# Block 1's seven-product units: three of the four weight sums made in DRAM by accumulating DMAs

## The chip, the cores and the metric

One core of one Trainium2 chip. The metric is device time of one execution, in microseconds (us).

## The reference, cut to what matters

Block 1 runs twice (l = 0, 1): a mixing part (latent attention "mla", a dilated attention "dil", a neighbourhood attention "nbr", gates, output projection) and then the feed-forward that the change is about. Block 2 follows and isn't touched.

```python
D_MODEL, SEQ, DEPTH = 1024, 512, 2
D_FF = 2816                      # 22 x 128
for l in range(DEPTH):
    ...                          # mixing part
    x = x + merged @ w_o[l]
    h = rms_norm(x, g_ffn[l])
    x = x + (jax.nn.silu(h @ w1[l]) * (h @ w3[l])) @ w2[l]
```

All is fp32. The kernel splits each operand in a high and a low part (fp32r) and makes a product as three matmuls: high x high, high x low, low x high.

## The kernel before, in words

**Engines and queues.** The program is written as one straight list per engine (TensorE, ScalarE, VectorE, GpSimd, SyncE); each executes its own in order, and waits on semaphores. A wait holds everything behind it on that engine.

**Weights.** All weights of the program lie in DRAM in one array `in_wts` of loads of 128 x 1024 (512 KB), in the order of use. SyncE loads them into slots of `s_raw` (2, and 4 in the feed-forward), each when its slot has been given back. A chunk is 1024 columns: ScalarE copies it to `wh` (high part, L611), VectorE subtracts to get `wl` (low part, L670), TensorE uses both. There are 3 slots of `wh` and `wl` (RING = 3), so chunk c can only be split when TensorE is done with chunk c - 3. `upto(L, c)`, `ahead()` and `weights()` say at which point of its list an engine puts the split of a chunk.

**The feed-forward of block 1.** 22 units i of 128 hidden columns. `KINDS` says how each is computed: 0 to 3 "U" (on the unnormalised x), 4 and 5 "N" (plain, on the normalised x: 48 matmuls of 512 columns each), 6 to 21 "S": the seven-product form, in which gate and up projection (w1 and w3, halves a and b of the 1024 inputs) share products over half of the tokens, 84 matmuls of 256 columns where a plain unit has 48 of 512. Units 0 to 10 come first, then half of w2 (`h_h`, `h_l` in the trace), then units 11 to 21, then the other half of w2.

An S unit has four chunks, made of two loads a = [w1a, w3a] and b = [w3b, w1b]:

- chunk 0: `s_b` = [w1a + w3a, w3a + w3b] (sum S1, 1024 wide, GpSimd, L714)
- chunk 1: [w1a, S2], with S2 = w1a + w3a + w3b, written over w3a in `s_raw` (512 wide, GpSimd, L714)
- chunk 2: w1b, 512 wide
- chunk 3: [w3b, S4], with S4 = S2 + w1b (512 wide, VectorE, L660, `s_raw<-s_raw`)

It needs four token sums too (`n_ta`, `n_tb`, split into `zh` and `zl`), made once per layer between the N units. GpSimd also makes the product of gate and up (`f_t<-f_t`, L714) of each U and S unit. In a unit ScalarE has in this order: copy c1, split of chunk 3, copy s1 (both copies write `s_s`); TensorE's product P2 waits for s1. Chunk 3's split waits for S4.

**The MLA loop.** 41 steps; in the first 32 TensorE makes a tile of scores, VectorE its minimum (L1427) and reciprocal (L1252), ScalarE the exponential (L614, `m_p<-bank`), GpSimd the scaling (`m_p<-m_p`, L717), and three steps later TensorE transposes that tile (L355). After it comes the dilated loop, 13 steps twice, whose first scaling on GpSimd is `b_p<-b_p` (L717).

## Time and profile before

| | us |
|---|---|
| median of 3 runs | 3257.82 (3256.49 to 3259.09) |
| the profiled execution | 3259.56 |
| its span in the trace | 3257.9 |

| engine | busy us | share |
|---|---|---|
| TensorE | 3203.1 | 98% |
| VectorE | 2030.9 | 62% |
| ScalarE | 1400.4 | 43% |
| GpSimd | 775.7 | 24% |

PE is TensorE, PEld its weight loads, DVE VectorE, ACT ScalarE, POOL GpSimd, SP SyncE. A matmul's end is modelled, so what counts is the distance from start to start. A share of busy time is a mean over stages with different limits; a hole in TensorE's row is read with the engine that released it, which stands in brackets. 40 slices of the span show a granted TensorE clock of 90% or more in each.

### The profile page before, as it was taken

The numbers are of one execution on the slowest core, as the hardware profiler recorded it, in microseconds if no ns is written. First come the engines' busy times: TensorE is split into PE (matmuls) and PEld (weight loads), VectorE is DVE, ScalarE is ACT, GpSimd is POOL, SyncE is SP. The second block draws the span as 40 slices with busy tenths as digits, with TensorE's granted clock in tenths as the row PEclk, the third lists the DMA queues.
The fourth block names the chain that finished last, engine by engine and source line by source line (L and its number), as shares of the span: only waits on it lengthen the run. The fifth ranks groups of instructions, "written<-read, shape, count | busy, mean of one in ns | idle before, by whom it ended". The sixth has DMA issues, their size and how long they took to land.

```text
span 3257.9 us, 41235 instructions
## 1 busy us (share of the span) xinstructions
PE 3203.1 (98%) x16588; PEld 2727.8 (84%) x16588; DVE 2030.9 (62%) x2980; ACT 1400.4 (43%) x2175; POOL 775.7 (24%) x562
## 2 busy tenths in 40 slices
PE   9999999999999999999999999999999999999998
PEld 7888888788888888888888888888888898788887
DVE  6865775777848655846949665554544268974433
ACT  5653553344437634633424433332423248843221
POOL 1521241223304311520325022110211013521101
PEclk9999999999999999999999999999999999999999
DMA  4122323232231122222222322222232222223322
GB/s 136 48 74 68 107 94 101 82 110 91 85 115 55 64 72 93 102 97 97 99 90 91 107 81 81 88 84 91 91 103 91 101 85 93 91 91 100 101 97 84
DMA packets 85150, 295.78 MB, mean 91 GB/s; under 512 B 9568, under 2 KB 12128, under 8 KB 84960
## 3 DMA queue, kind: packets, MB, share of 16 engines
q1 hardware_dynamic: 84384, 292.76, 27.0%
q8 instruction: 131, 2.15, 0.3%
q14 instruction: 59, 0.48, 0.0%
q10 hardware_dynamic: 576, 0.40, 0.0%
HBM read 291.02 MB, written 2.10 MB: 90 GB/s over the span
## 4 chain that ended last, share of the span: by engine, by line
PE 78%; DVE 13%; ACT 4%; issue 3%; POOL 2%; DMA 0%; SPq 0%; ACTq 0%; POOLq 0%; DVEq 0%
PE bank L352 77%; DVE wl L670 5%; PE bank L355 2%; ACT wh L611 1%; DVE s_raw L660 1%; ACT m_p L614 1%; DVE small L1427 1%; POOL f_t L714 1%; POOL u_g L714 1%; DVE f_t L660 1%; DVE u_uc L666 0%; DVE m_ptl L670 0%; DVE h_l L673 0%; DMA s_raw<-in_wts 0%; DVE m_qf L660 0%
## 5 line engine op out<-in xcount | busy, mean ns | idle before, releaser
L670 DVE TENSOR_TENSOR wl<-s_raw,wh 128x1024 fp32r<-128x1024 f32 (+1 forms) x563 | 734.1, 1308 | 552.2 <-ACT wh L611 551.1
L352 PE MATMUL bank<-zh,wh 128*128 128x512 f32 (+1 forms) x2588 | 946.9, 366 | 5.7 <-ACT zh L611 5.7
L352 PE MATMUL bank<-zh,wl 128*128 128x512 f32 (+1 forms) x2588 | 942.4, 364 | 5.0 <-DVE wl L670 5.0
L352 PE MATMUL bank<-zl,wh 128*128 128x512 f32 (+1 forms) x2588 | 939.8, 363 | 1.7 <-DVE zl L673 1.6
L611 ACT ACTIVATE wh<-s_raw 128x1024 fp32r<-128x1024 f32 (+1 forms) x563 | 575.1, 1028 | 550.2 <-PE bank L352 410.1
L352 PEld LDWEIGHTS bank<-zh,wl 128*128 128x128 f32 x2588 | 489.1, 189 | 88.7 <-DVE wl L670 11.4
L352 PEld LDWEIGHTS bank<-zh,wh 128*128 128x128 f32 x2588 | 489.6, 189 | 80.2 <-ACT zh L611 5.7
L352 PEld LDWEIGHTS bank<-zl,wh 128*128 128x128 f32 x2588 | 489.3, 189 | 75.8 <-DVE zl L673 3.0
L714 POOL TENSOR_TENSOR f_t<-f_t 128x512 f32<-128x512 f32 x84 | 118.1, 1406 | 524.7 <-DVE f_t L666 524.7
L720 POOL TENSOR_TENSOR small<-small 128x1 f32<-128x1 f32 (+3 forms) x35 | 43.0, 1229 | 822.1 <-DVE small L663 822.1
L352 PE MATMUL bank<-n_h,wh 128*128 128x256 f32 (+1 forms) x448 | 136.9, 306 | 24.9 <-ACT s_s L611 17.6
L352 PE MATMUL bank<-f_mh,wh 128*128 128x512 f32 (+1 forms) x396 | 146.4, 370 | 0.0
L352 PE MATMUL bank<-wh,zh 128*128 128x512 f32 (+2 forms) x384 | 145.1, 378 | 1.0 <-ACT b_qk L611 1.0
L714 POOL TENSOR_TENSOR s_b<-s_raw 128x1024 f32<-128x1024 f32 x32 | 84.7, 2645 | 256.2 <-DMA s_raw<-in_wts 219.8
L352 PE MATMUL bank<-f_mh,wl 128*128 128x512 f32 (+1 forms) x396 | 145.3, 367 | 0.0
L352 PE MATMUL bank<-f_ml,wh 128*128 128x512 f32 (+1 forms) x396 | 144.2, 364 | 0.0
L352 PE MATMUL bank<-wh,zl 128*128 128x512 f32 (+2 forms) x384 | 143.8, 375 | 0.0
L352 PE MATMUL bank<-wl,zh 128*128 128x512 f32 (+2 forms) x384 | 143.7, 374 | 0.0
L614 ACT ACTIVATE f_t<-f_t 128x512 f32<-128x512 f32 x84 | 53.0, 631 | 208.2 <-DVE f_t L660 208.2
L352 PE MATMUL bank<-h_h,wl 128*128 128x512 f32 x352 | 138.7, 394 | 0.0
L352 PE MATMUL bank<-n_h,wl 128*128 128x256 f32 (+1 forms) x448 | 134.4, 300 | 3.7 <-DVE wl L670 3.7
L352 PE MATMUL bank<-h_l,wh 128*128 128x512 f32 x352 | 138.0, 392 | 0.0
(379 smaller groups left out, 5849.8 us busy)
## 6 DMA issues: line engine op xcount, KB each, us to landing
s_raw<-in_wts SPq DMA_DIRECT2D x529, 512.0 KB, 3.3
c_nb<-in_c_bias SPq DMA_DIRECT2D x16, 384.0 KB, 3.1
x<-in_xT SPq DMA_DIRECT2D x8, 256.0 KB, 5.7
out<-x SPq DMA_DIRECT2D x13, 128.0 KB, 1.8
b_mask<-in_b_mask SPq DMA_DIRECT2D x2, 576.0 KB, 3.7
r_d<-in_decay SPq DMA_DIRECT2D x4, 256.0 KB, 2.6
s_raw<-in_wts SPq DMA_DIRECT2D x2, 256.0 KB, 3.7
m_t<-in_mla_tab SPq DMA_DIRECT2D x2, 256.0 KB, 4.6
```

Source lines behind the costliest of these rows:

```text
L352: return self.e.matmul(out, l, r, start=start, stop=stop, skip_group_check=inside)
L355: return self.e.transpose(out, in_, self.m.ident)
L611: return self.e.activation(out, in_, ACT.Copy, scale=scale)
L614: return self.e.activation(out, in_, func, **kw)
L660: return self.e.tensor_tensor(out, a, b, op)
L670: return self.e.tensor_tensor(out, src, b32(hi), ALU.subtract)
L714: return self.e.tensor_tensor(out, a, b, op)
L720: return self.e.tensor_tensor(out, v, self.m.negh[:, 0:n], ALU.pow)
L1427: L.e.tensor_reduce(m.mn[:, c:c + 1], m.bank[4 + i % 2], AX.X, ALU.min).then_inc(*L.tell("mn", "mla", l, i))
```

## The change

Three of the four sums of a unit (both halves of S1, and S2) are no longer made by GpSimd on the chip. GpSimd issues DMAs for them in the mixing part of the same layer: `weight_sums` is a generator that gives out one "turn" at the end of each step of the three attention loops, and each turn waits for the DMAs of the turn before. Per unit there are two copies from `in_wts` to a new DRAM array `sums` (512 and 256 KB), then two accumulating DMAs of 256 KB (S3 and S1 in the code), then one of 256 KB (S2): five DMAs in three turns, 80 in 48 turns per layer. SyncE loads `s_b` and the S2 half of chunk 1 from `sums`. S4 stays on VectorE. In the N units the splits of the weight chunks are put ahead of the token sums or between them, and the first token differences move from i = 3 to i = 2.

```diff
@@ -332,13 +332,13 @@
-    def load(self, sem="wl"):
+    def load(self, unit=None):
         self.book.plan.append([])
-        self.book.loads.append((slot, self.held.get(slot, self.first)))
-        self.held[slot] = sem, "rel", n
+        self.book.loads.append((slot, self.held.get(slot, self.first), unit))
+        self.held[slot] = "wl", "rel", n
         return n
@@ -381,11 +381,11 @@
-    def s_loads(self):
+    def s_loads(self, unit):
         self.slot = (self.slot + self.slot % 2) % self.slots
-        return [self.load(), self.load()]
+        return [self.load(("a",) + unit), self.load(("b",) + unit)]
@@ -636,10 +636,10 @@
         if part == 0:
-            self.wait_ge("pl", "S1", *unit)
+            self.wait_ge("rawb", *unit)
             self.cp(wh, m.s_b).then_inc(*self.tell("wh", c))
         elif part == 1:
-            self.wait_ge("pl", "S2", *unit)
+            landed(self, a)
             self.cp(wh, src[:, 0:1024]).then_inc(*self.tell("wh", c))
@@ -702,7 +702,6 @@
             self.wait_ge("wl", c)
-            self.wait_ge("pl", "S2", *unit)
             self.tt(src[:, 1536:2048], src[:, 512:1024], src[:, 1536:2048], ALU.add).then_inc(
@@ -727,10 +726,30 @@
         m = self.m
-        slot, after = self.book.loads[n]
+        slot, after, unit = self.book.loads[n]
         if after:
             self.wait_ge(*after)
+        if unit:
+            self.load_s(n, slot, *unit)
+            return
         self.e.dma_start(m.raw[slot], m.A["wts"][n]).then_inc(*self.tell(f"raw{slot}", n, by=16))
+    def load_s(self, n, slot, side, *unit):
+        m, wts, sums = self.m, self.m.A["wts"], s_sums(self.m, unit)
+        f, l, i = unit
+        self.wait_ge("sa", "S2", *unit)
+        if side == "a":
+            self.e.dma_start(m.raw[slot][:, 0:512], wts[n][:, 0:512]).then_inc(*self.tell(f"raw{slot}", "x", n, by=16))
+            self.e.dma_start(m.raw[slot][:, 512:1024], sums[:, 1024:1536]).then_inc(*self.tell(f"raw{slot}", n, by=16))
+            return
+        self.e.dma_start(m.raw[slot], wts[n]).then_inc(*self.tell(f"raw{slot}", n, by=16))
+        before = (f, l, i - 1) if KINDS[i - 1] == "S" else (f, 0, FF - 1) if l else None
+        if before:
+            self.wait_ge("wl", self.book.s_at(0, before))
+        else:
+            self.wait_ge("mm", "acc", f, l, 0, 0)
+        self.e.dma_start(m.s_b, sums[:, 0:1024]).then_inc(*self.tell("rawb", *unit, by=16))
@@ -1130,6 +1149,7 @@
     gpsimd_q(L, l, 0)
+    L.sums = weight_sums(L, l)
@@ -1462,6 +1482,7 @@
             gpsimd_y(L, m.m_yf, *m.ya, (i - 14) // 8, (i - 14) // 8, "mla", l)
+        sum_turn(L)
@@ -1852,6 +1873,7 @@
                 gpsimd_b(L, ("b", l, 1) + n)
+        sum_turn(L)
@@ -2121,6 +2143,7 @@
                 gpsimd_proj(L, l, 1, n)
+        sum_turn(L)
@@ -2394,7 +2417,7 @@
     unit = F + (i,)
-    loads = L.s_loads()
+    loads = L.s_loads(unit)
     tile = lambda w, k: (("w1", "w3")[w], (l,), 128 * k, range(128 * i, 128 * i + 128))
@@ -2621,21 +2644,55 @@
-def gpsimd_sums(L, F, i):
-    unit = F + (i,)
-    book = L.book
-    a, b = book.ring[book.s_at(0, unit)][3:]
-    src = L.m.s_raw[book.loads[a][0] // 2]
-    landed(L, a)
-    landed(L, b)
-    before = F + (i - 1,) if KINDS[i - 1] == "S" else ("f", 0, FF - 1) if F[1] else None
-    if before:
-        L.wait_ge("wl", book.s_at(0, before))
-        L.wait_ge("pl", "S2", *before)
-    L.tt(L.m.s_b, src[:, 0:1024], src[:, 512:1536], ALU.add).then_inc(*L.tell("pl", "S1", *unit))
-    L.wait_ge("pl", "S1", *unit)
-    L.tt(src[:, 512:1024], L.m.s_b[:, 512:1024], src[:, 0:512], ALU.add).then_inc(*L.tell("pl", "S2", *unit))
+def s_units():
+    return [i for i in range(FF) if KINDS[i] == "S"]
+def s_sums(m, unit):
+    f, l, i = unit
+    units = s_units()
+    return m.A["sums"][len(units) * l + units.index(i)]
+def weight_sums(L, l):
+    book, wts, units = L.book, L.m.A["wts"], s_units()
+    last = None
+    def add(to, x, *key):
+        L.e.dma_start(to, x, accum_op=ALU.add).then_inc(*L.tell("sa", *key, by=16))
+    def of(k):
+        unit = ("f", l, units[k])
+        return (unit, s_sums(L.m, unit)) + tuple(book.ring[book.s_at(0, unit)][3:5])
+    for k in range(len(units) + 2):
+        if k < len(units):
+            unit, s, a, b = of(k)
+            if last:
+                L.wait_ge("sa", *last)
+            L.e.dma_start(s[:, 0:1024], wts[a]).then_inc(*L.tell("sa", "c0", *unit, by=16))
+            L.e.dma_start(s[:, 1024:1536], wts[a][:, 0:512]).then_inc(*L.tell("sa", "c1", *unit, by=16))
+            last = ("c1",) + unit
+            yield
+        if 0 < k <= len(units):
+            unit, s, a, b = of(k - 1)
+            L.wait_ge("sa", *last)
+            add(s[:, 0:512], wts[a][:, 512:1024], "S3", *unit)
+            add(s[:, 512:1024], wts[b][:, 0:512], "S1", *unit)
+            last = ("S1",) + unit
+            yield
+        if 1 < k:
+            L.wait_ge("sa", *last)
+            unit, s, a, b = of(k - 2)
+            add(s[:, 1024:1536], s[:, 512:1024], "S2", *unit)
+            last = ("S2",) + unit
+            yield
+def sum_turn(L):
+    next(L.sums, None)
@@ -2727,19 +2784,25 @@
 FIRST_S = KINDS.index("S")
-TOKEN_SUMS = {4: (0, 1, 2), 5: (3,)}
     m, nxt, F = L.m, after_ffn1(l), ("f", l)
+    c = L.book.s_at(0, F + (FIRST_S,))
     scalar_rows(L, ("ffn", l))
             scalar_half_mid(L, F, l, i - 1)
-        for j in TOKEN_SUMS.get(i, ()):
-            scalar_token_sum(L, F, j)
-            L.ahead()
+        if i == 4:
+            upto(L, c - 2)
+            scalar_token_sum(L, F, 0)
+            scalar_token_sum(L, F, 1)
+            upto(L, c - 1)
+            scalar_token_sum(L, F, 2)
+        if i == 5:
+            scalar_token_sum(L, F, 3)
+            upto(L, c)
         if KINDS[i] == "N":
@@ -2758,6 +2821,7 @@
     m, nxt, F = L.m, after_ffn1(l), ("f", l)
+    c = L.book.s_at(0, F + (FIRST_S,))
     vector_stat(L, ("ffn", l))
@@ -2771,9 +2835,15 @@
             vector_half_mid(L, F, i - 1)
-        for j in TOKEN_SUMS.get(i, ()):
-            vector_token_sum(L, F, j)
-            L.ahead()
+        if i == 4:
+            upto(L, c - 2)
+            vector_token_sum(L, F, 0)
+            vector_token_sum(L, F, 1)
+            upto(L, c - 1)
+            vector_token_sum(L, F, 2)
+        if i == 5:
+            vector_token_sum(L, F, 3)
+            upto(L, c)
         if KINDS[i] == "N":
@@ -2782,7 +2852,7 @@
             vector_normed(L, F, range(4 * i - 4, 4 * i))
-        if i == 3:
+        if i == 2:
             vector_token_sums(L, F)
@@ -2799,16 +2869,13 @@
-    gpsimd_sums(L, F, units[0])
     for i in units:
-        if i + 1 in units:
-            gpsimd_sums(L, F, i + 1)
-        if i - 1 in units:
-            gpsimd_unit(L, F, i - 1)
-    gpsimd_unit(L, F, units[-1])
+        gpsimd_unit(L, F, i)
 def gpsimd_ffn1(L, l):
+    for _ in L.sums:
+        pass
     gpsimd_stat(L, ("ffn", l))
@@ -4253,6 +4320,7 @@
         A["wts"] = nc.dram_tensor("in_wts", (len(book.plan), 128, 1024), F32, kind="ExternalInput").ap()
+        A["sums"] = nc.dram_tensor("sums", (2 * len(s_units()), 128, 1536), F32, kind="Internal").ap()
         two_blocks(nc, m, book, ctx)
```

## Rows read from the trace of the kernel before

**Rows 1.** The page's busy line, whole span.

```profile
PE 3203.1 (98%) x16588; PEld 2727.8 (84%) x16588; DVE 2030.9 (62%) x2980; ACT 1400.4 (43%) x2175; POOL 775.7 (24%) x562
```

**Rows 2.** Busy time by stretch: from:to, length, then each engine, clock, DMA.

```profile
614.78:625.73 10.95, 10.95 (x49) 8.83 (x47) 10.95 (x10) 2.21 (x3) 7.16 (x3) 1.00 0.30 96
...
614.78:647.42 32.64, 25.73 (x97) 20.09 (x96) 24.72 (x22) 10.67 (x13) 11.97 (x5) 0.84 0.20 65
647.42:657.43 10.01, 10.01 (x85) 10.00 (x84) 8.36 (x12) 5.49 (x9) 1.14 (x1) 1.00 0.33 106
647.42:699.95 52.53, 50.59 (x421) 50.17 (x420) 49.05 (x60) 28.50 (x45) 18.05 (x10) 1.00 0.31 103
760.39:880.49 120.10, 112.17 (x926) 110.55 (x925) 113.87 (x131) 61.86 (x97) 50.13 (x28) 1.00 0.27 89
1545.61:1573.80 28.19, 24.06 (x98) 19.04 (x97) 24.31 (x22) 10.80 (x13) 9.70 (x4) 0.94 0.23 75
1573.80:1626.98 53.18, 51.02 (x422) 50.29 (x420) 49.87 (x60) 28.39 (x45) 21.04 (x12) 1.00 0.30 101
1687.42:1809.03 121.61, 112.92 (x926) 110.79 (x925) 113.65 (x129) 61.28 (x96) 52.85 (x28) 1.00 0.27 88
67.12:149.47 82.35, 80.83 (x458) 67.56 (x456) 71.03 (x139) 60.01 (x126) 49.90 (x46) 1.00 0.14 46
```

**Rows 3.** TensorE in order of time, between the two N units: start, length, idle before.

```profile
631.24 0.76 PE L352 MATMUL bank<-n_h,wh 128*128 128x512 f32 x1 [5.29 <-ACT wh L611]
...
634.04 0.80 PE L352 MATMUL bank<-n_h,wl 128*128 128x512 f32 x1 [1.61 <-DVE wl L670]
```

**Rows 4.** VectorE in order of time, ahead of that hole.

```profile
621.71 2.89 DVE L670 TENSOR_TENSOR h_l<-f_t,h_h 128x512 fp32r<-128x512 f32 x1
```

**Rows 5.** A unit in order of time: GpSimd, ScalarE, VectorE, TensorE.

```profile
668.24 2.40 POOL L714 TENSOR_TENSOR s_b<-s_raw 128x1024 f32<-128x1024 f32 x1 [4.62 <-DMA s_raw<-in_wts]
...
672.99 1.06 ACT L611 ACTIVATE wh<-s_raw 128x1024 fp32r<-128x1024 f32 x1 [2.96 <-DVE s_raw L660]
...
668.95 2.24 DVE L670 TENSOR_TENSOR wl<-s_raw,wh 128x512 fp32r<-128x512 f32 x1
671.23 1.67 DVE L660 TENSOR_TENSOR s_raw<-s_raw 128x512 f32<-128x512 f32 x1
...
674.37 0.39 PE L352 MATMUL bank<-n_h,wh 128*128 128x256 f32 x1 [1.00 <-ACT s_s L611]
```

**Rows 6.** The same two VectorE instructions in the first unit, GpSimd idle.

```profile
648.97 0.68 DVE L670 TENSOR_TENSOR wl<-s_raw,wh 128x512 fp32r<-128x512 f32 x1
649.68 0.69 DVE L660 TENSOR_TENSOR s_raw<-s_raw 128x512 f32<-128x512 f32 x1
```

**Rows 7.** GpSimd in order of time: first and last MLA scaling, first dilated one.

```profile
67.12 0.70 POOL L717 TENSOR_SCALAR m_p<-m_p,small 128x512 f32<-128x512 f32 x1 [9.32 <-DVE small L1252]
...
149.47 0.70 POOL L717 TENSOR_SCALAR m_p<-m_p,small 128x512 f32<-128x512 f32 x1
...
180.11 0.91 POOL L717 TENSOR_SCALAR b_p<-b_p,small 128x768 f32<-128x768 f32 x1 [22.34 <-DVE small L1252]
```

**Rows 8.** DMA issues (KB, median us to landing); tile s_raw: issue ns, landing.

```profile
r_d<-in_decay SPq DMA_DIRECT2D x4, 256.0 KB, 2.6
...
L733 SPq DMA_DIRECT2D s_raw<-in_wts x528: 327/328/444, 7.7 to 3221.0; - x176
...
DMA to landing us min/median/max: 2.8/3.3/7.3
```

**Rows 9.** TensorE's transposes of scaled tiles: the first, and the first dilated.

```profile
68.49 0.60 PE L355 MATMUL bank<-ident,m_p 128*128 128x128 f32 x4
...
181.20 0.81 PE L355 MATMUL bank<-ident,b_p 128*128 128x128 f32 x6
```

**Rows 10.** GpSimd: the second dilated scaling.

```profile
185.54 0.91 POOL L717 TENSOR_SCALAR b_p<-b_p,small 128x768 f32<-128x768 f32 x1 [4.52 <-DVE small L1252]
```

**Rows 11.** GpSimd: an instruction on a tile of 128 x 4.

```profile
582.00 1.02 POOL L720 TENSOR_TENSOR small<-small 128x4 f32<-128x4 f32 x1 [52.92 <-DVE small L663]
```

More of the change, by code:

```diff
@@ L62 @@
     "pw", "sc", "pl",
-    "rawf", "raw0", "raw1", "raw2", "raw3", "cst0", "cst", "idn", "tab", "rct", "kct", "msk", "cb0", "cb1", "dec", "ret", "out", "out2",
+    "rawf", "raw0", "raw1", "raw2", "raw3", "rawb", "sa", "cst0", "cst", "idn", "tab", "rct", "kct", "msk", "cb0", "cb1", "dec", "ret", "out", "out2",
 ) + tuple(f"xi{i}" for i in range(8))
```

## The prediction, made before the change was run

> **What bounds the kernel now.** I read first the page's busy line: TensorE 98% of 3257.9 us, VectorE 62%, GpSimd 24% [rows 1]. So only places where TensorE stands, or runs at half clock, can be won; only places where it now runs without a hole can be lost. Next the table by stretch [rows 2]. In both blocks the two non-shared units before the seven-product units (96 matmuls) and the seven-product units themselves are longer than their matmuls need. Last, the order of the instructions in one place of each kind, and in the attention, where the new work goes.
>
> The two plain units: their first 48 matmuls take 10.95 us, 0.228 us each. All 96 take 32.64 us in layer 0 and 28.19 in layer 1 [rows 2], against 2 x 10.95 = 21.9. TensorE waits 5.29 us for ScalarE's half of a weight chunk and 1.61 for VectorE's [rows 3], and for part of the stretch it has the lower of its clocks (granted 0.84 over it, [rows 2]). Above it lies a VectorE queue of token sums, in which a 512-wide instruction took 2.89 us while GpSimd made the first weight sum; the like without it takes 0.68 [rows 4, 6].
>
> The units: the first runs without a hole in 10.01 us [rows 2], so 16 need 160.2. They take 52.53 + 120.10 = 172.6 in layer 0 and 53.18 + 121.61 = 174.8 in layer 1. The holes are of one form [rows 5]: TensorE waits 1.00 us for an s_s copy of ScalarE; ScalarE had stood 2.96 us, until VectorE's sum in s_raw; and that came late since VectorE's two half-width instructions took 2.24 and 1.67 us beside GpSimd's s_b and s_raw sums. Without GpSimd beside them the same two take 0.68 and 0.69 [rows 6].
>
> **Part by part.** (1) GpSimd's 64 sums in the feed-forward go. In a unit VectorE gets back (2.24 - 0.68) + (1.67 - 0.69) = 2.5 us ahead of the chunk that was late, more than the hole of 1.0 to 1.2. Next late would be VectorE's own queue: it was busy 8.36 of 10.01 us in the first unit [rows 2], so nothing. I take the whole excess: 172.6 - 160.2 + 174.8 - 160.2 = 27.0 us. GpSimd's product of gate and up remains beside VectorE; it was there in the first unit too (GpSimd 1.14 us busy, [rows 2]).
>
> (2) The plain units. The token differences move one unit forward, and the chunk that was late is now split ahead of the token sums. Its slot has been free since TensorE began the first plain unit (614.78, [rows 2]), so it can be ready about 622, before 625.7. The second follows two token sums, near 628, needed 5.5 us after 625.7. Excess 32.64 + 28.19 - 2 x 21.9 = 17.0 us, all of it taken. Parts 1 and 2 give 44.0 us if all goes well, half of that at least.
>
> (3) SyncE's loads. A unit now loads 1.5 MB instead of 1 MB, in four DMAs for two, each 0.33 us on SyncE [rows 8]. The s_b load is issued when VectorE has made the low half of the previous unit's first chunk, and ScalarE wants it three of four chunks, so some 7 us, later; a 512 KB load lands in 3.3 us, 7.3 at most [rows 8]. Behind it in SyncE's queue are the next loads, and their slots come free later still. DMA share 0.3 in the units [rows 2]. Cost nothing; if that cover were gone, the loads' lateness would stand in each unit.
>
> (4) GpSimd in the attention. This decides. Per layer 80 DMAs in 48 turns: 16 turns of two copies (512 and 256 KB), 16 of two accumulates of 256 KB, 16 of one. One turn ends each step of the MLA loop (41), then of the dilated loop; the rest is done after seven of these. Each turn but the first begins with a wait for the DMAs of the turn before, and it stands in GpSimd's own queue. Behind it is queued the scaling of the next softmax tile (m_p), TensorE's transposes wait for that, and behind them the scores of the next step.
>
> That loop has no room. Its 32 scalings start between 67.12 and 149.47, so 82.35/31 = 2.66 us apart [rows 7]; the first transposes come 0.67 us behind the first scaling's end [rows 9], and TensorE is busy 80.8 of 82.35 us [rows 2]. If a turn takes T from its issue to its landing, and T is over 2.66, then 30 steps per layer go at T instead. From the last scaling to the first one of the dilated attention there are 30.6 us [rows 7], and 11 turns are between: 11T - 30.6 more. Those transposes follow the first dilated scaling by 0.2 us, so the delay is passed on [rows 7, 9]. The next dilated scaling is 5.4 us after the first [rows 7, 10], so the last six waits cost nothing up to about T = 5. Both layers, the second taken like the first: 2 x (30(T - 2.66) + 11T - 30.6) = 82T - 220.8 us.
>
> What is T? No DMA of GpSimd, none from DRAM to DRAM, and no accumulate is in the trace. The nearest rows: a 256 KB load lands 2.6 us after issue, one of 512 KB 3.3, the least ever 2.8 [rows 8]. So 0.7 per 256 KB on top of 1.9. Lower bound, everything as a plain load and GpSimd's part free: 4.0, 3.3 and 2.6 us, mean 3.3; with all at their least, 0.5 below: 2.8. Middle: an accumulate reads two operands, so it counts double: 4.0, 4.7, 3.3, mean 4.0; and GpSimd makes its part of each DMA as an instruction, for which I take its price for a tiny one, 1.02 us [rows 11], before the data can move: T = 5.0. Upper bound: accumulates at a quarter of the load rate (7.5 and 4.7), writes to DRAM at half (6.1), and all 1.67 DMAs of a turn at 1.02 one after the other: 6.1 + 1.7 = 7.8. I take 5.0, since no reason makes an accumulate in DRAM as cheap as a load into the chip's own memory.
>
> The Trainium skill (DMA: Bandwidth & Descriptors, Anatomy of one DMA, the GpSimd path) gives such a DMA 2.0 us plus its bytes at 436 GB/s. That is an estimate of 3.8, 3.2 and 2.6, mean 3.2, and the sum would then be 82 x 3.2 - 220.8 - 44 = -2 us: no change. No run here shows it yet; its figure is for loads from DRAM to the chip, as are my rows.
>
> Sum: 82 x 5.0 - 220.8 = 189.2 lost, 44.0 won, net +145.2. The profiled execution took 3259.6 (span 3257.9), the median is 3257.8: 3405 against the one, 3403 against the other.
>
> **The rivals.** A, the other side, faster: the wait in the turn is short. The break-even is 82T = 264.8, T = 3.2 us. At 2.8 it costs 9 us against 44: 3223. For it: two loads of three sizes land near that. Against: a copy of 512 + 256 KB alone is over it at the load rate. B, no change: T = 3.2 to 3.3, 3255 to 3264; for it the mean of plain loads, 3.3, against it that accumulates must read more. By the page of the Trainium skill named above this rival would be the likeliest. C, heavier: T = 7.8, lost 419, and in the dilated loop six turns per layer of some 2 us over its step, 24 more: 3657. For it: nothing in the trace bounds an accumulate from above. D, the change doesn't do what it says: the units' holes stay, since the low chunk waits on something else (in layer 1 some holes wait for VectorE's wl, not for s_s). That is 27 us less won: 3430 with T = 5.
>
> **How the numbers follow.** Forecast with D inside (T 3.8 to 6.5, 3305 to 3550): 0.62. C: 0.13. B: 0.09. A: 0.16. Range: A and the upper part of C left out, 3250 to 3620. A measurement of this kernel tells 0.2% (6.5 us) from no change: faster 0.16, same 0.09, slower 0.75.
>
> **What would show it.** Right: the m_p scalings 5 us apart instead of 2.66, and TensorE waiting for GpSimd there, busy some half of the stretch; GpSimd's queue waiting for DMAs of sums; the first dilated scaling 25 us later against the last MLA one; the 96 plain matmuls in about 22 us and the units at 10.0 each, with VectorE's half-width wl at 0.68. Wrong: scalings still near 2.7 apart (then T is small, and the result is A); turns that land in under 3.2; holes in the units in front of an s_s copy still, or ScalarE waiting for an s_b load; a lower granted clock in the MLA stretch, which I did not price, since at half clock 2.66 us of matmuls become about 5, within a step of T.

## The result, and the profile after

| | before | after |
|---|---|---|
| median | 3258.45 us (3256.49 to 3261.07) | 3453.82 us (3453.47 to 3454.18) |
| span of the profiled execution | 3257.9 | 3451.7 |
| ratio after/before | | 1.0599, 95% interval 1.0581 to 1.0617 |

The kernel is 195 us slower. Both halves of the forecast are in the trace: the feed-forward's units became 40 us shorter, and what lies ahead of them, nearly all of it in the attention, 235 us longer.

The page of the kernel after: the busy line, three rows of its 40 slices, the chain that ended last by line, a queue, and the landing times of the new DMAs.

```profile
PE 3246.8 (94%) x16588; PEld 2751.4 (80%) x16588; DVE 1957.9 (57%) x2980; ACT 1411.2 (41%) x2175; POOL 745.6 (22%) x658
...
PE   8667999999998667999999999999999999999998
...
POOL 1544123110102533123110102111111012441101
PEclk9988999999999988999999999999999999999999
...
q0 software_dynamic: 20992, 50.34, 7.4%
...
PE bank L352 77%; DMA sums<-in_wts 8%; DMA sums<-sums 3%; PE bank L355 1%; DVE wl L670 1%; POOL f_t L713 1%; POOL u_g L713 1%; POOL sums L2664 1%; DMA s_raw<-in_wts 1%; POOL sums L2675 0%; DVE c_kl L670 0%; ACT wh L611 0%; DVE u_uc L666 0%; DVE u_t L666 0%; DVE c_q L670 0%
...
sums<-in_wts POOLq DMA_DIRECT2D x96, 256.0 KB, 4.7
sums<-in_wts POOLq DMA_DIRECT2D x32, 512.0 KB, 3.6
...
sums<-sums POOLq DMA_DIRECT2D x32, 256.0 KB, 4.2
```

Counted from 0, TensorE leaves its 9s in slices 0 to 3 and 12 to 15 only (and in the last one, as before): the MLA loops and what lies between them and the dilated loops. 11% of the chain is now DMAs of `sums`, which were in no chain before. TensorE's share falls from 98% to 94% although GpSimd is busy no longer than before (22%, before 24%, [rows 1]): GpSimd isn't working more, it stands.

The waits of the kernel after (who waits, for whom, us in total, times, longest):

```profile
POOL sums L2664 <- DMA sums<-in_wts: 171.6, 55, 9.5
...
PE bank L355 <- POOL m_p L716: 97.3, 58, 4.6
...
POOL sums L2675 <- DMA sums<-sums: 69.7, 26, 4.3
```

GpSimd waits 241 us for its own DMAs, and TensorE's transposes wait 97 us for GpSimd's scaling. GpSimd in order of time in layer 0's MLA loop, three turns of the sums, and TensorE's transposes in the same stretch:

```profile
84.58 0.57 POOL L2675 DMA_DIRECT2D sums<-in_wts  x1 [3.99 <-DMA sums<-in_wts]
85.15 0.56 POOL L2676 DMA_DIRECT2D sums<-in_wts  x1
85.72 0.72 POOL L716 TENSOR_SCALAR m_p<-m_p,small 128x512 f32<-128x512 f32 x1
86.38 1.31 POOL L713 TENSOR_TENSOR b_qk<-b_qk,b_rc 128x512 f32<-128x512 f32 x1
89.07 1.75 POOL L2664 DMA_DIRECT2D sums<-in_wts  x2 [1.38 <-DMA sums<-in_wts]
90.25 1.67 POOL L716 TENSOR_SCALAR m_p<-m_p,small 128x512 f32<-128x512 f32 x1
91.90 1.26 POOL L713 TENSOR_TENSOR m_ql<-m_qf,m_qh 128x512 fp32r<-128x512 f32 x1
95.68 0.84 POOL L2664 DMA_DIRECT2D sums<-sums  x1 [2.52 <-DMA sums<-in_wts]
```

```profile
86.58 0.63 PE L355 MATMUL bank<-ident,m_p 128*128 128x128 f32 x4 [1.32 <-POOL m_p L716]
...
92.07 0.63 PE L355 MATMUL bank<-ident,m_p 128*128 128x128 f32 x4 [2.78 <-POOL m_p L716]
```

Each scaling stands right behind a turn's issue, the next turn waits for the landing of the last, and the transposes follow: 86.58 to 92.07, 5.5 us, where the loop before had 2.66 per step [rows 7].

Layer 0's MLA loop, layer 1's and the stretch from the last MLA scaling to the first dilated one, then the plain units of both layers and the seven-product units of layer 0 (layer 1's take 50.09 and 110.22 us) (from:to, length, busy time of each engine, clock, DMA share, GB/s), to be read against [rows 2]:

```profile
66.64:225.14 158.50, 108.03 (x501) 83.04 (x499) 78.67 (x145) 66.06 (x130) 83.59 (x99) 0.89 0.57 126
1088.94:1250.74 161.80, 106.75 (x501) 83.51 (x499) 78.57 (x145) 65.60 (x130) 83.19 (x99) 0.91 0.57 124
225.14:287.12 61.98, 27.54 (x133) 23.93 (x133) 15.49 (x30) 15.49 (x28) 15.01 (x20) 0.71 0.60 141
...
726.77:749.58 22.81, 22.34 (x97) 18.03 (x97) 18.22 (x20) 11.38 (x14) 1.30 (x1) 1.00 0.33 116
1758.17:1782.91 24.74, 24.27 (x97) 19.26 (x97) 19.12 (x20) 11.38 (x14) 1.28 (x1) 0.93 0.35 117
749.58:799.67 50.09, 50.09 (x421) 50.09 (x420) 41.45 (x61) 29.08 (x45) 5.20 (x4) 1.00 0.46 149
860.11:970.32 110.21, 110.21 (x925) 110.21 (x924) 88.66 (x131) 63.85 (x97) 13.00 (x10) 1.00 0.44 140
```

The whole difference by stretch, in us (layer 0, layer 1; stretches are cut at starts of the same instructions in both traces):

| stretch | before | after | difference |
|---|---|---|---|
| first to last MLA scaling | 82.35, 82.40 | 158.50, 161.80 | +76.2, +79.4 |
| to the first dilated scaling | 30.64, 29.43 | 61.98, 67.64 | +31.3, +38.2 |
| to the 15th dilated scaling | 141.60, 141.62 | 145.34, 145.10 | +3.7, +3.5 |
| to the first plain unit | 293.07, 293.06 | 294.31, 294.69 | +1.2, +1.6 |
| two plain units | 32.64, 28.19 | 22.81, 24.74 | -9.8, -3.5 |
| seven-product units | 172.6, 174.8 | 160.3, 160.3 | -12.3, -14.5 |

235.1 lost, 40.1 won, 195.0 net; the spans differ by 193.8. The loss ahead of the first plain unit isn't the attention's: e3 and e4 below show most of it too, and it belongs to the new order.

### The profile page after: what moved, and what is told of

Read it like the earlier page. It is cut to its first block, busy times and chain, and to the rows that moved or that the text cites. A ratio compares the mean times of both kernels' runs of the same rounds, so it can differ in the third digit from the quotient of the medians.

```text
span 3451.7 us, 41380 instructions
## 1 busy us (share of the span) xinstructions
PE 3246.8 (94%) x16588; PEld 2751.4 (80%) x16588; DVE 1957.9 (57%) x2980; ACT 1411.2 (41%) x2175; POOL 745.6 (22%) x658
## 4 chain that ended last, share of the span: by engine, by line
PE 79%; DMA 12%; DVE 4%; POOL 2%; issue 2%; ACT 1%; SPq 0%; ACTq 0%; POOLq 0%; DVEq 0%
PE bank L352 77%; DMA sums<-in_wts 8%; DMA sums<-sums 3%; PE bank L355 1%; DVE wl L670 1%; POOL f_t L713 1%; POOL u_g L713 1%; POOL sums L2664 1%; DMA s_raw<-in_wts 1%; POOL sums L2675 0%; DVE c_kl L670 0%; ACT wh L611 0%; DVE u_uc L666 0%; DVE u_t L666 0%; DVE c_q L670 0%
## 5 line engine op out<-in xcount | busy, mean ns | idle before, releaser
L670 DVE TENSOR_TENSOR wl<-s_raw,wh 128x1024 fp32r<-128x1024 f32 (+1 forms) x563 | 686.1, 1223 | 564.9 <-ACT wh L611 563.7
L352 PE MATMUL bank<-f_mh,wl 128*128 128x512 f32 (+1 forms) x396 | 145.3, 367 | 0.0
L355 PE MATMUL bank<-ident,m_p 128*128 128x128 f32 x256 | 44.2, 300 | 101.6 <-POOL m_p L716 97.3
L352 PE MATMUL bank<-h_h,wh 128*128 128x512 f32 x352 | 136.6, 388 | 0.0
L352 PE MATMUL bank<-n_h,wh 128*128 128x256 f32 (+1 forms) x448 | 133.8, 299 | 2.2 <-ACT wh L611 2.2
```

The costliest lines, as they stand in the source:

```text
L352: return self.e.matmul(out, l, r, start=start, stop=stop, skip_group_check=inside)
L355: return self.e.transpose(out, in_, self.m.ident)
L670: return self.e.tensor_tensor(out, src, b32(hi), ALU.subtract)
```

## The experiments

All but e4 start from the kernel after. The table has what they measured; the stretches are those above, and "reach" is how many turns back the DMAs were issued for which a turn waits. (With a reach of 4, three turns stand between; the expectations of e9 and e11 count those three. A turn of copies then waits for nothing.)

| run | turns of the sums | reach | us | MLA | to dilated | dilated | to plain |
|---|---|---|---|---|---|---|---|
| after | 41 in the MLA loop, 7 in the dilated one | 1 turn | 3453.8 | 158.5, 161.8 | 62.0, 67.6 | 145.3, 145.1 | 294.3, 294.7 |
| e1 | the same | 4 turns | 3242.4 | 86.8, 86.2 | 35.6, 35.8 | 141.6, 141.6 | 294.3, 294.8 |
| e2 | every second MLA step | 1 | 3264.9 | 88.2, 88.0 | 33.9, 36.0 | 153.4, 152.1 | 294.3, 295.0 |
| e3 | none | - | 3220.6 | 82.4, 83.1 | 29.4, 29.4 | 141.6, 141.6 | 294.3, 294.4 |
| e5 | as after, copies for accumulates | 1 | 3372.5 | 132.3, 133.8 | 51.9, 51.0 | 145.6, 145.5 | 294.3 |
| e7 | as after, a quarter of the columns | 1 | 3314.5 | 111.6, 111.7 | 42.5, 45.0 | 145.4, 145.7 | 294.3 |
| e6 | dilated and neighbourhood loops | 4 | 3245.0 | 82.3, 83.1 | 33.0, 31.6 | 141.6, 141.6 | 304.2, 302.5 |
| e8 | the same | 1 | 3279.7 | 82.4, 83.1 | 32.3, 31.6 | 152.3, 150.1 | 313.0, 311.4 |
| e9 | dilated loops and output projection | 4 | 3233.3 | 82.4, 83.1 | 32.0, 31.6 | 141.6, 141.6 | 297.4, 298.0 |
| e11 | feed-forward, from unit 0 | 4 | 3228.2 | 82.3, 83.1 | 30.5, 29.4 | 141.6, 141.6 | 297.3, 295.7 |
| e12 | six in the dilated loop, rest from unit 3 | 4 | 3255.1 | 82.3, 83.1 | 30.7, 29.4 | 141.6, 141.6 | 297.0, 295.9 |

**e1_far_wait: the same DMAs in the same places, another wait.** Two sets of semaphores for each kind of turn, so that a turn waits for what it needs itself, issued four turns before, and not for the turn just before it.

```diff
-            L.wait_ge("sa", *last)
-            add(s[:, 0:512], wts[a][:, 512:1024], "S3", *unit)
...
+            sem = sum_sem("d", k - 1)
+            L.wait_ge(sum_sem("c", k - 1), "c1", *unit)
+            add(sem, s[:, 0:512], wts[a][:, 512:1024], "S3", *unit)
...
-            L.wait_ge("sa", *last)
...
-            add(s[:, 1024:1536], s[:, 512:1024], "S2", *unit)
...
+            L.wait_ge(sum_sem("d", k - 2), "S1", *unit)
...
+            add(sum_sem("e", k - 2), s[:, 1024:1536], s[:, 512:1024], "S2", *unit)
```

> The changed kernel, but each turn waits only for the DMAs whose result it uses (issued four turns before), with a semaphore of its own for each group in flight, and not for those of the turn before. Same DMAs, same places. Theory 'wait' (the loss is GpSimd standing in front of its own scalings until the previous turn's DMAs land, 5.1 to 5.2 us): the waits vanish, the MLA step falls from 5.1 to about 2.9 (GpSimd's 1.6 us of work per step plus 1.25 of issuing), and the time is 3230 us (3215 to 3245), faster than before. Rival 'issue' (GpSimd's time for making the DMAs is what fills the step) or rival 'traffic' (the DMAs' bytes slow the loads or the DRAM): the step stays near 5 and the time near 3450.

Measured: 3242.36 us (3241.69 to 3243.66), ratio to before 0.995 [0.9934, 0.9967]. 211 of the 233 us that separate after from e3 are gone, with all 160 DMAs still made, in fewer microseconds. Its MLA loop of layer 0 by window, and GpSimd there:

```profile
66.89:153.66 86.77, 82.93 (x466) 68.11 (x464) 74.24 (x139) 60.19 (x126) 82.60 (x100) 1.00 0.96 226
```

```profile
85.05 1.55 POOL L716 TENSOR_SCALAR m_p<-m_p,small 128x512 f32<-128x512 f32 x1
86.56 1.71 POOL L2668 DMA_DIRECT2D sums<-in_wts  x2
88.39 1.05 POOL L716 TENSOR_SCALAR m_p<-m_p,small 128x512 f32<-128x512 f32 x1
```

The DMA engines are busy 96% of this loop and TensorE is slowed by 4.4 us of 82.4. So it was not traffic; it was the wait in GpSimd's queue. What is left is GpSimd's own: it is busy 82.6 of 86.8 us, with no sums 49.8 of 82.4. So the 7.6 us that e1 loses in the two MLA loops are, by this, the price of issuing the DMAs in a loop that has no room.

The 12.5 us that it loses behind the two loops are another matter, and there traffic does cost. The two weight loads that SyncE issues there (in the windows 161:164 of e1, then 158.2:161 of e3) land much later beside GpSimd's DMAs:

```profile
s_raw<-in_wts SPq DMA_DIRECT2D x2, 512.0 KB, 11.2
...
s_raw<-in_wts SPq DMA_DIRECT2D x2, 512.0 KB, 5.4
```

The first of them, issued at 161.69, landed at 172.30, 10.6 us later (4.8 in e3). ScalarE started on it at once; the copies to `b_q` and `b_k` stood behind that in its list, and TensorE behind those:

```profile
172.39 1.06 ACT L611 ACTIVATE wh<-s_raw 128x1024 fp32r<-128x1024 f32 x1 [5.73 <-PE bank L352]
```

```profile
176.91 0.76 PE L352 MATMUL bank<-b_k,b_q 128*128 128x512 f32 x1 [4.62 <-issue]
```

(The bracket of ScalarE's row names TensorE, but ScalarE started 0.09 us after the landing.) Behind the hole the granted clock was 0.61 (176.91 to 184.00). Layer 1 has the same hole, 4.1 us. e3 has neither, and in the attention it differs from e1 by these DMAs alone.

**e2_every_second: half of the turns in the MLA loop.** The wait as in after.

```diff
-        sum_turn(L)
+        if i % 2:
+            sum_turn(L)
```

> The changed kernel with a turn at every second MLA step only, all waits kept; the other turns come in the dilated loop. Theory 'wait': two steps of 2.66 us are 5.3, as long as a turn takes (5.15), so the MLA stage nearly keeps its old 82 us, six turns lie in the 30.6 us before the dilated scalings, and the 26 dilated steps of 5.4 to 7.8 us cost a few us: 3242 us (3225 to 3270). Rival 'issue': half of the loss in the MLA loop stays, about 3350.

Measured: 3264.94 us (3256.57 to 3266.33), ratio 1.0016 [1.0007, 1.0025]. One turn of 5 us fits in two steps of 2.66: the loop lost 5.9 us instead of 76. The turns that now fall in the dilated loop, 26 of them, cost 11.7 there. So that loop's slack is smaller than [rows 7, 10] made me think: a turn in each of its steps does cost, some 0.4 us a step.

**e3_no_sums: no DMA of sums at all.** The units take weights that were not summed (loads of the same sizes from `in_wts`), so the sums are left out of the computation.

```diff
-    L.sums = weight_sums(L, l)
+    L.sums = iter(())
```

> The changed kernel without any of GpSimd's DMAs: SyncE's four loads per unit stay, but read the plain weights, so the three sums of every unit are left out. It shows what the feed-forward part wins by itself. By the stretches of the changed kernel's trace (plain units 9.8 and 3.5 us shorter, the seven-product units 12.3 and 14.5): 3258 - 40 = 3218 us (3212 to 3224). If the loads from the sums array or the larger traffic had cost the units something, it would be lower still.

Measured: 3220.56 us (3218.86 to 3222.17), 0.9884 [0.9869, 0.9899]. This is the whole prize: 38 us, where 44 were forecast. The price of the sums in after is 233 us.

**e4_order_only: the kernel before, with the new order in the plain units and nothing else of the change.**

```diff
-        for j in TOKEN_SUMS.get(i, ()):
...
+        if i == 4:
+            upto(L, c - 2)
+            vector_token_sum(L, F, 0)
...
-        if i == 3:
+        if i == 2:
             vector_token_sums(L, F)
```

> The kernel before with the other part of the change alone: in the plain units the chunk splits ahead of or between the token sums, the differences one unit earlier; GpSimd's sums stay. Theory 'order' (the late chunk was queued behind the token sums): most of the 13.3 us that these units won comes, 3248 us (3245 to 3252). Rival 'port' (VectorE's instructions were long beside GpSimd's first sum, and that made the hole): 3255 us (3252 to 3258).

Measured: 3255.09 us (3254.01 to 3260.05), 0.9991 [0.9982, 1.0001]. The total fits the reading that the order is worth nothing while GpSimd makes sums. By stretch it is otherwise: the plain units took 24.23 and 24.61 us, so the order wins 8.4 and 3.6 there. The first five seven-product units then took 55.86 and 56.54, where before had 52.53 and 53.18, and give 6.7 of it back. In them TensorE still waits for `s_s`, the hole of [rows 5]:

```profile
646.75 0.38 PE L352 MATMUL bank<-n_h,wh 128*128 128x256 f32 x1 [1.32 <-ACT s_s L611]
```

The order also has a price of its own. With it the first plain matmul waits 1.1 us for ScalarE's chunk, in after, e3 and e4 alike, and not in the kernel before or in e10. This is after's:

```profile
726.77 0.47 PE L352 MATMUL bank<-n_h,wh 128*128 128x512 f32 x1 [1.10 <-ACT wh L611]
```

**e10_old_order: e3 with the plain units in the old order.** The sums are left out here too.

```diff
-        if i == 4:
-            upto(L, c - 2)
-            vector_token_sum(L, F, 0)
...
+        for j in {4: (0, 1, 2), 5: (3,)}.get(i, ()):
+            vector_token_sum(L, F, j)
+            L.ahead()
```

> No sums are made anywhere (the units take unsummed weights, all other work stays), as in e3_no_sums, but the plain units have the old order: token differences at unit 3, token sums ahead of the weight chunks. It tells what part of the gain in the plain units is the order's and what GpSimd's absence. Theory (order): the excess of the plain units stays, 32.6 and 28.2 us in place of 22.8 and 24.4, less what VectorE's token sum of 2.89 us takes longer beside GpSimd (2.2 us at most, layer 0): 10 to 13 us over e3_no_sums, 3230 to 3234. Rival (port): the token sums were late only because GpSimd's first weight sum ran beside VectorE: both stretches near 23 to 25, 3221 to 3224.

Measured: 3227.67 us (3227.49 to 3228.40), 0.9908 [0.9893, 0.9923]. The hole between the two plain units is there in both layers, with GpSimd doing nothing beside it:

```profile
613.51:641.70 28.19, 24.07 (x98) 19.07 (x97) 21.45 (x22) 10.68 (x13) 2.21 (x1) 0.94 0.35 112
1528.17:1556.41 28.24, 24.12 (x98) 19.05 (x96) 21.55 (x22) 10.79 (x13) 2.21 (x1) 0.94 0.31 112
```

```profile
626.70 0.47 PE L352 MATMUL bank<-n_h,wh 128*128 128x512 f32 x1 [2.02 <-ACT wh L611]
629.51 0.80 PE L352 MATMUL bank<-n_h,wl 128*128 128x512 f32 x1 [2.10 <-DVE wl L670]
```

e4 and e10 split the 13.3 us won in the plain units. Old order without sums: 28.2 in both layers; new order: 22.8 and 24.4. So 9.2 us are the order's where no sums are made (12.0 in e4, where they are; the two causes overlap). The other part is what GpSimd's first sum cost in layer 0 under the old order (32.64 to 28.19, 4.5 us; in layer 1 nothing). Of the 9.2, the order gives 2.7 back ahead of the plain units (294.3 and 294.4 in e3, 293.0 in both layers of e10), which is why e10's time falls between the two forecasts: the order is worth 7.1 us of time.

**e5_copies: each accumulate made as a plain copy of the same bytes.** The sums are left out, the DMAs are as many and as large.

```diff
-        L.e.dma_start(to, x, accum_op=ALU.add)...
+        L.e.dma_start(to, x)...
```

> The changed kernel with its three accumulating DMAs per unit issued as plain copies of the same bytes from GpSimd (so the sums are left out), all waits and turns kept. It splits the length of a turn. In the changed kernel a turn of two copies is followed by the next 4.7 us later, one of two accumulates 6.5, one of one 4.5. Theory 'an accumulate reads twice': the second falls to about 5.0 and the third to 3.7, the mean turn from 5.2 to 4.4, and with 82 us of time per us of turn the kernel takes 3453 - 65 = 3388 us (3360 to 3415). Rival 'the path is slow, not the adding': turns stay at 5 and the time over 3435.

Measured: 3372.47 us (3371.19 to 3373.99), 1.0349 [1.0333, 1.0365], inside the range of the theory.

**e7_quarter: all five DMAs of a unit on a quarter of their columns**, 128 and 64 KB; accumulates stay accumulates. Three quarters of each sum are left out, and the units take weights that were not summed.

```diff
-            add(s[:, 0:512], wts[a][:, 512:1024], "S3", *unit)
-            add(s[:, 512:1024], wts[b][:, 0:512], "S1", *unit)
+            add(s[:, 0:128], wts[a][:, 512:640], "S3", *unit)
+            add(s[:, 128:256], wts[b][:, 0:128], "S1", *unit)
```

> The changed kernel with a quarter of the columns in each of GpSimd's DMAs, five per unit as before, all waits and turns kept; SyncE loads plain weights instead of the sums, so the sums are left out. It measures the part of a turn that is not bytes. Theory 'a turn is 1.0 us of GpSimd plus 1.9 fixed plus bytes at 0.7 us per 256 KB': a mean of about 3.2 us, close to break-even: 3218 + 82 x 3.2 - 221 = 3260 us (3245 to 3285). If the fixed part is larger (4 us or more), 3325 and more: then smaller transfers would not have saved the change.

Measured: 3314.52 us (3312.87 to 3316.27), 1.0172 [1.0158, 1.0186]. The forecast of 3260 missed: T is 3.60, where it had 3.2, and a microsecond of T costs more than 82. e5 and e7 take a turn apart. Its length in us, from its issue to the issue of the next one where that had to wait, medians:

| turn | after | e5, copies | e7, quarter |
|---|---|---|---|
| two copies, 512 + 256 KB | 4.7 | 4.9 | 3.4 |
| two accumulates, 256 KB each | 6.4 | 4.6 | 4.1 |
| one accumulate, 256 KB | 4.5 | 3.3 | 3.0 |
| time per MLA step, mean | 5.17 | 4.29 | 3.60 |

An accumulate costs over a copy 1.8 us for the pair and 1.2 for the single one. Three quarters of the bytes cost 1.3 to 2.3. The 3.0 to 4.1 us that are left in e7 are mostly not a matter of size. Against the three times per step, the loss over e3 is 233, 152 and 94 us: 84 to 92 us per microsecond, where I had 82.

**e6_far_late and e8_near_late: no turn in the MLA loop**, the wait of e1 or of after.

```diff
@@ gpsimd_mla
-        sum_turn(L)
```

> A version that may beat both: the far waits of the run before (each turn waits only for what it uses), and no turn in the MLA loop; 26 turns in the dilated loops, 21 in the neighbourhood loop, one after. The far-wait run lost 4.4 and 3.8 us in the MLA loop and 5 and 6.4 behind it, against the run without the DMAs, and nothing in the dilated loops; without MLA turns those 20 us go: 3223 us (3219 to 3232). If the neighbourhood loop is as tight on GpSimd as the MLA loop (two scalings per step of 5.6 us), a few us come back there.

> The changed kernel with its near waits (each turn waits for the turn before), but no turn in the MLA loop. It tells the place from the wait. Theory 'a wait costs only what a turn is longer than the step it stands in': dilated steps of 4.9 to 7.8 us against turns of 4.5 to 6.5 cost 5 to 10 us per layer (the changed kernel lost 3.7 with six of them), neighbourhood steps of 5.6 some more: 3240 us (3228 to 3265). Rival 'any near wait in front of a scaling costs its whole landing': over 3300.

Measured: e6 3245.01 us (3241.67 to 3249.11), 0.9959 [0.9946, 0.9971]; e8 3279.73 us (3276.57 to 3282.39), 1.0065 [1.0051, 1.0079]. Both leave the MLA loop as it was. The dilated loop takes a turn per step for nothing if the wait reaches far (141.6) and for 10.7 and 8.5 us if it doesn't. The neighbourhood loop, which got the other 22 turns, has no room either: 9.9 and 8.0 us with the far wait, 18.7 and 17.0 with the near one. e6 is no better than e1, and 22 us over its forecast: I moved the work from one tight loop to another. e8 misses its range too, for the same reason, but its rival, over 3300, is out.

**e9_loose: the far wait, 26 turns in the dilated loops, the rest three at a time behind the GpSimd parts of the output projection.**

```diff
@@ gpsimd_out
         (behind each of the eight parts)
+            for _ in range(3):
+                sum_turn(L)
```

> All sums made, each turn waits for a turn three places back (as in e1_far_wait), and the turns stand only where the runs so far showed TensorE's work to have room on GpSimd's side: 26 in the two dilated loops, one per step, and three behind each of the eight GpSimd parts of the output projection; none in the MLA loop, none in the neighbourhood loop. Theory (a turn costs what it adds to GpSimd's queue in a place where GpSimd's next instruction is due, and nothing elsewhere; the DMAs' traffic itself costs nothing): MLA 82.4 and 83.1 us, tail 29.4, last dilated scaling to the plain units 294.3 to 297, so 3221 to 3228 us: as with no sums at all, up to 7 us for the output projection. Rival 1 (the output projection is as tight as the neighbourhood loop, which cost 8 to 10 us per layer in e6_far_late): 302 to 304 there, 3238 to 3241. Rival 2 (the traffic in DRAM beside SyncE's loads costs, wherever it is): 3235 or more, with TensorE waiting for pieces that hang on s_raw.

Measured: 3233.25 us (3231.61 to 3235.37), 0.9926 [0.9913, 0.9938], 9 us better than e1 and between the theory and its first rival: 2.6 and 2.2 us went before the first dilated scaling, 3.1 and 3.6 in the projection. The former is the second rival, traffic, in small: one turn of copies stands there, SyncE's weight load beside it landed 7.5 us after its issue (4.8 in e3), ScalarE waited 2.56 us for it, and TensorE 1.45.

**e11_in_ffn: no turn in the attention. Three behind each product of gate and up, in the feed-forward that uses the sums.** GpSimd had 13 us of work in 110 there.

```diff
@@ gpsimd_units, gpsimd_ffn1
         gpsimd_unit(L, F, i)
+        for _ in range(3):
+            sum_turn(L)
```

> All sums made, each turn waiting three places back, but no turn in the attention or the output projection at all: three turns (five DMAs) stand on GpSimd behind each product of gate and up in the feed-forward itself, from unit 0 on, so the sums of unit 6 + k are finished behind unit k + 1, some 40 us before they are used. Theory (only GpSimd's queue in tight loops matters): attention as in the kernel before (82.4 and 83.1, tail 29.4, 293.0), units at 50.1 and 110.2, plain units 22.8 to 24.4: 3219 to 3223 us, the time without any sums. Rival 1 (the issue of a DMA on GpSimd, 0.55 to 0.89 us each, slows VectorE beside it as GpSimd's own sums did, where 0.68 us became 2.24): five issues, some 3.7 us in a unit, and the holes come back in part: units over 10.0 us each in the windows, up to the 27 us of the kernel before for both layers, 3235 to 3248. Rival 2 (the sums' traffic beside SyncE's loads, which are densest here): s_raw or s_b late, TensorE waiting for ScalarE behind a load, over 3240.

Measured: 3228.16 us (3224.99 to 3229.17), 0.9906 [0.989, 0.9923]: faster than both kernels, and 7.6 us from having no sums at all. The units took 51.2, 110.3, 51.1 and 110.4 us, 2.5 us over e3 in all. The time lies between the theory and the first rival. GpSimd, then VectorE, between layer 0's plain units and in its second seven-product unit:

```profile
626.64 0.55 POOL L2676 DMA_DIRECT2D sums<-in_wts  x1
627.17 1.76 POOL L2665 DMA_DIRECT2D sums<-in_wts  x2
...
659.31 1.48 POOL L2665 DMA_DIRECT2D sums<-sums  x1
```

```profile
626.84 0.69 DVE L670 TENSOR_TENSOR h_l<-f_t,h_h 128x512 fp32r<-128x512 f32 x1 [2.07 <-ACT h_h L611]
...
659.95 1.22 DVE L670 TENSOR_TENSOR wl<-s_b,wh 128x1024 fp32r<-128x1024 f32 x1
```

Beside the issue of these DMAs VectorE makes `h_l` in 0.69 us, where the same instruction took 2.89 beside GpSimd's first weight sum [rows 4]. All four such `h_l` of this run, and 12 of 128 x 1024 from `s_b` (1.22 us each), take as long as with GpSimd idle: issuing DMAs doesn't hold VectorE up as the sums did. The largest part of the 7.6 us stands ahead of the plain units, and is the old mechanism in small. A turn waited 3.83 us, the product of gate and up stood behind it at 603.03, and behind that ScalarE and its next weight chunk:

```profile
601.90 1.73 POOL L2665 DMA_DIRECT2D sums<-in_wts  x2 [3.83 <-DMA sums<-in_wts]
603.03 1.93 POOL L713 TENSOR_TENSOR f_t<-f_t 128x512 f32<-128x512 f32 x1
```

```profile
604.99 0.63 ACT L611 ACTIVATE h_h<-f_t 128x512 fp32r<-128x512 f32 x1 [4.31 <-POOL f_t L713]
605.53 1.04 ACT L611 ACTIVATE wh<-s_raw 128x1024 fp32r<-128x1024 f32 x1
```

**e12_split: e11 without the turns behind units 0 to 2**; six go to the end of the dilated loop, and each sum is finished one unit later than in e11.

```diff
@@ gpsimd_ffn1
-        for _ in range(3):
+        for _ in range(3 if i > 2 else 0):
             sum_turn(L)
@@ gpsimd_dil
+        if p == 1 and i > 6:
+            sum_turn(L)
```

> As e11_in_ffn, but the turns behind units 0 to 2 of the feed-forward are taken away, where a turn that waited 3.83 us stood ahead of a product of gate and up that ScalarE's list waits for, with a new weight chunk behind it, and TensorE had holes of 1.5 and 1.5 us (606 and 618 us). Six turns go in the last six steps of the second dilated loop, which have no scaling behind them; from unit 3 on three turns stand behind each product. Theory (the 3.0 and 1.3 us that e11_in_ffn has between the last dilated scaling and the plain units are such waits): that stretch 294.3 and 294.4 as without sums, 3220 to 3224 us in all, 4 to 7 less than e11_in_ffn. Rival (the loss there is the traffic's, or the GpSimd issue's in the first units wherever the turns begin): it moves behind unit 3 and the time stays at 3226 to 3229.

Measured: 3255.10 us (3252.97 to 3260.49), 0.9994 [0.9985, 1.0003]. Both readings fell. The stretch ahead of the plain units stayed at 297.0 and 295.9: the hole before 606.62 went, and others, 2.7 us in all, came within 38 us of the last dilated scaling, where the six turns stand (a weight load beside them landed 11.4 us after its issue, 5.5 in e3). And the units lost 28 us over e11, since the sums came too late. In layer 0 the last sum of unit 10 was issued at 659.75; SyncE, which waits for it, issued that unit's first load at 670.52 and the `s_b` load at 672.88, and ScalarE waited until 684.62:

```profile
684.62 1.06 ACT L611 ACTIVATE wh<-s_b 128x1024 fp32r<-128x1024 f32 x1 [6.73 <-DMA s_b<-sums]
```

```profile
685.72 0.38 PE L352 MATMUL bank<-zh,wh 128*128 128x256 f32 x1 [3.08 <-ACT wh L611]
```

A DMA of the sums lands late in both runs (10.8 us after its issue here, 11.6 in e11, 4.2 in after: medians of the last accumulates), with four others of its queue ahead of it; e12 has one unit less to cover that. In e11 the unit's first load was issued at 664.94 and `s_b`'s at 672.22; `s_b` landed after 8.2 us, ScalarE waited 2.46 us for it, and TensorE not at all. In e12 `s_b` was issued only 0.7 us later but took 11.7 us. There the unit's four loads, 1.5 MB, are issued within 2.4 us, in e11 within 7.3. That this crowding made `s_b` land late is argued, not shown.

## Why the prediction was right, and where its terms were off

The forecast was 3403 us with a range of 3250 to 3620; measured 3453.8. The mechanism is the one that was named, and e1 shows it: the same DMAs without the near wait cost 22 us instead of 233. The sum is off by 50 us: 4 too much won, 46 too little lost.

**The units (27.0 forecast).** Measured 26.8. All 32 run at 10.02 us each without a hole. VectorE's two half-width instructions beside them take 0.69 and 0.69 us, as in [rows 6]. Rival D is out. The Trainium skill (SBUF — State Buffer, SBUF: two separate sides) says that a VectorE instruction with two inputs in SBUF and a GpSimd instruction that reads SBUF hold one pair of ports in turn, each for its whole length, and that DMAs use other ports; the 2.24 us before, the 0.69 after and the 0.69 beside DMAs in e11 agree with both halves: in [rows 5] the instruction of 2.24 us ends at 671.19, about its own 0.68 after GpSimd's sum does at 670.64.

**The plain units (17.0 forecast).** Measured 13.3. I took both stretches down to 21.9; they are 22.8 and 24.7. In layer 1 the granted clock is 0.93 over the stretch, where layer 0 has 1.00: the 96 matmuls are there busy 24.27 us, in layer 0 22.34. That the holes had two causes was in the prediction, but not how they divide: the order 9.2, GpSimd's sum 4.5 (e10). Nor was the order's price of 2.7 us ahead of the units.

**SyncE's loads (0 forecast).** 0: `s_b` lands 3.6 us after issue (median), ScalarE never waits for it in after. The cover is thin all the same: in e12, whose sums landed late, it was gone, and that run lost 28 us. And the term had only the loads in the units: in e1, e6, e8 and e9 it's SyncE's loads in the attention that GpSimd's DMAs make late.

**The length of a turn (T = 5.0 forecast).** Measured 5.11 and 5.22 us per MLA step. That the mean came so close is in part luck, as the make-up was off more. GpSimd's part of a DMA is 0.55 us for a copy and 0.83 to 0.89 for an accumulate, not 1.02 [rows 11]. The copies took 4.7 (I had 4.0 + 1.0), the accumulate pair 6.4 (4.7 + 1.0), the single one 4.5 (3.3 + 1.0). That an accumulate should count double was right in direction: 1.8 and 1.2 us over a copy (e5).

The Trainium skill's 2.0 us plus bytes at 436 GB/s (DMA: Bandwidth & Descriptors, Anatomy of one DMA, the GpSimd path) gave the estimates of 3.8, 3.2 and 2.6 us and a result within 2 us of before. The measured 4.7, 6.4 and 4.5, from issue to next issue, are 0.9, 3.2 and 1.9 over it; as plain copies (e5) 4.9, 4.6 and 3.3 still 0.7 to 1.4 over. From issue to landing a single 256 KB copy takes 3.0 us in e5, 0.4 over. For these DMAs the measurement decides. So rivals A and B, which needed T up to 3.3, had no ground. With a quarter of the bytes T was still 3.6.

**The cost per T (82T - 220.8 forecast).** This is the step that was mis-sized most. Put T = 5.17 in it and it gives 203 us; measured against e3 233. The MLA loop itself is nearly right: 31 steps at 5.17 are 160, measured 158.5 and 161.8; the prediction let only 30 of them go at T, which is 5 of the 30 us for both layers. The tail, from the last MLA scaling to the first dilated one, is not. GpSimd in order of time behind the last MLA scaling:

```profile
225.14 0.71 POOL L716 TENSOR_SCALAR m_p<-m_p,small 128x512 f32<-128x512 f32 x1
228.84 1.73 POOL L2664 DMA_DIRECT2D sums<-in_wts  x2 [2.99 <-DMA sums<-in_wts]
238.95 0.81 POOL L2664 DMA_DIRECT2D sums<-sums  x1 [8.38 <-DMA sums<-in_wts]
...
286.55 0.80 POOL L2664 DMA_DIRECT2D sums<-sums  x1 [4.55 <-DMA sums<-in_wts]
287.12 1.18 POOL L716 TENSOR_SCALAR b_p<-b_p,small 128x768 f32<-128x768 f32 x1
```

The 11 turns that I counted are there, but they take 5.7 us each, not 5.2: the one issued at 228.84 takes 10.1, the three other accumulate pairs behind it 6.2 to 7.0. Beside the long one SyncE loads 1.6 MB, issued from 228.01 to 229.74 and the last landed at 237.57; in layer 1 such a turn stands beside the same loads and takes 11.2. That the loads made it long was not tested. The stretch is 62.0 and 67.6 us, where 11T makes 57 at T = 5.17. That is 17 of the 30 us; the dilated loop is 7 more. Behind the tail TensorE had stood in one piece:

```profile
288.35 1.54 PE L355 MATMUL bank<-ident,b_p 128*128 128x128 f32 x6 [22.84 <-POOL b_p L716]
```

**The dilated loop (0 up to T = 5 forecast).** 3.7 and 3.5 us. The reading of [rows 10] was too kind: e2 and e8 lost 8.5 to 11.7 us there with a near wait in each step.

**The break-even (T = 3.2 forecast).** The line through after, e5 and e7 falls to the 38 us that were won at about T = 3.0. No turn of these runs was that short in the mean.

**The clock in the MLA loop, which I didn't price.** The prediction gave a lower clock as a sign that it would be wrong, and it came: granted 0.89 and 0.91 there and 0.71 in the tail. I find no term for it: the turns follow one another without a gap, so a step is as long as its turn, and TensorE waits for GpSimd at the end of it. No run held the clock apart from the holes, so that it cost nothing there is argued, not shown. TensorE was busy 68% of the first loop, where the prediction had some half.

## What to carry to other kernels

A wait costs what stands behind it in its queue, not what it waits for. The same 160 DMAs in the same places cost 233 us when each turn waited for the one before, and 22 when it waited for the one four back; in the feed-forward, whose GpSimd work had slack, they cost 8. So before an engine is given a side job, look at what each step of its loop has queued behind the place, and let the job's waits reach back further than its latency. What is left then is the time of the issues themselves, and traffic: another engine's loads beside these DMAs land late (10.6 us for 4.8 in e1), so look for a load that is due there. And a side job has a due time as well: one unit less of lead turned a gain of 0.9% into none.

## What the runs showed of the hardware that I had not expected

- An accumulate from GpSimd, from DRAM to DRAM, took 3.0 us from issue to the next issue in a chain of waits even at 64 KB (e7), with 0.83 us of it on GpSimd's own queue (0.55 for a copy).
- An accumulate costs time over a copy of the same bytes: 1.2 us for 256 KB, 1.8 for two of them (after against e5).
- DMA engines busy 96% of the MLA loop at 226 GB/s left TensorE's clock at 1.00 and its busy time at 82.9 of 86.8 us (e1). Behind the loop the same traffic did cost: a weight load landed 10.6 us after its issue, where it took 4.8 without GpSimd's DMAs (e3), and TensorE stood 4.6 us for it.
- GpSimd's DMA issue doesn't slow VectorE's instructions with two inputs (0.69 us for `h_l`, e11), while GpSimd's arithmetic made the same instruction take 2.89 [rows 4].
